# Stick-breaking values moved by one token: five transfers instead of two, and their differences ahead of the attention barrier

## The reference, cut to what matters

```python
log_keep = jnp.where(strict, jax.nn.log_sigmoid(-z), 0.0)
suffix = lax.cumsum(log_keep, axis=log_keep.ndim - 1, reverse=True) - log_keep
a = jnp.where(strict, jnp.exp(jax.nn.log_sigmoid(z) + suffix), 0.0)
return jnp.einsum('bhqs,bhsd->bhqd', a.astype(vh.dtype), vh)
```

## Time and profile before

| | us |
|---|---|
| median of 3 runs | 2915.65 |
| lowest and highest | 2914.1 and 2923.84 |
| profiled execution, its time | 2925.78 |
| profiled execution, its span | 2924.0 |
| PE busy in the span | 2787.3 (95%) |
| DVE busy | 1969.0 (67%) |
| ACT busy | 1158.3 (40%) |
| POOL busy | 99.9 (3%) |

### The profile page before, as it was taken

The page is one execution under the profiler, slowest core; times in us unless marked ns, Lnnn a source line. Parts: engine busy times, 40 slices in busy tenths (PEclk is TensorE's granted clock), DMA queues, the critical chain, the costliest instruction groups (busy, mean ns, idle before and its releaser), DMA issues.

```text
span 2924.0 us, 39546 instructions
## 1 busy us (share of the span) xinstructions
PE 2787.3 (95%) x15525; PEld 2269.3 (78%) x15525; DVE 1969.0 (67%) x3222; ACT 1158.3 (40%) x2049; POOL 99.9 (3%) x109
## 2 busy tenths in 40 slices
PE   6999988998999999999999999899979999999999
PEld 4878865677888776878888888778658788888887
DVE  6435215677446665487777787689975877777885
ACT  4334216633237785343333344411153433333443
POOL 1030001010320000000000000000000000000000
PEclk8999999998999998999999999899989999999999
DMA  7020210024100002222323563211002323325632
GB/s 282 17 85 22 65 38 15 10 93 128 43 12 2 2 1 94 93 96 106 116 102 107 206 223 101 65 51 44 17 30 99 105 101 108 115 101 206 223 94 101
DMA packets 187010, 257.31 MB, mean 88 GB/s; under 512 B 29736, under 2 KB 138700, under 8 KB 182220
## 3 DMA queue, kind: packets, MB, share of 16 engines
q1 hardware_dynamic: 182672, 232.45, 24.2%
q10 hardware_dynamic: 4155, 22.35, 1.9%
HBM read 186.62 MB, written 67.11 MB: 87 GB/s over the span
## 4 chain that ended last, share of the span: by engine, by line
PE 69%; DVE 7%; ACT 1%; issue 1%; DMA 0%; ACTq 0%; DVEq 0%
PE ps L1658 28%; PE ps L1666 14%; PE ps L1611 11%; PE ps L1434 4%; PE ps L1537 2%; PE ps L1488 2%; PE ps L1506 2%; PE ps L1722 2%; PE ps L1151 1%; PE ps L1773 1%; PE ps L1030 1%; PE ps L1759 0%; PE ps L1412 0%; DMA ring<-in_ffn_w_gate_dram 0%; DVE ht L2937 0%
## 5 line engine op out<-in xcount | busy, mean ns | idle before, releaser
L1658 PE MATMUL ps<-x_ops,w_ring 128*128 128x512 f32 x3696 | 841.9, 390 | 6.8 <-ACT even_rows L2287 5.3
L1658 PEld LDWEIGHTS ps<-x_ops,w_ring 128*128 128x128 f32 x3696 | 694.2, 188 | 152.6 <-issue 8.4
L1666 PE MATMUL ps<-a_ring,w_ring 128*128 128x512 f32 x1848 | 419.3, 389 | 0.0
L1666 PEld LDWEIGHTS ps<-a_ring,w_ring 128*128 128x128 f32 x1848 | 346.8, 188 | 72.2 <-DVE w_ring L3041 0.2
L1611 PE MATMUL ps<-h_high,ring_parts 128*128 128x512 f32 x1024 | 319.1, 393 | 19.0 <-DVE h_low L2509 9.8
L2229 ACT ACTIVATE w_ring<-ring 128x512 fp32r<-128x512 f32 x230 | 144.1, 628 | 302.7 <-PE ps L1658 284.8
L2472 DVE TENSOR_TENSOR ring_parts<-ring,ring_parts 128x1024 fp32r<-128x1024 f32 (+2 forms) x77 | 95.3, 1240 | 219.5 <-ACT ring_parts L1858 218.9
L1611 PEld LDWEIGHTS ps<-h_high,ring_parts 128*128 128x128 f32 x1024 | 192.6, 189 | 64.5 <-issue 12.9
L1611 PE MATMUL ps<-h_low,ring_parts 128*128 128x512 f32 x512 | 200.3, 391 | 0.0
L1858 ACT ACTIVATE ring_parts<-ring 128x1024 fp32r<-128x1024 f32 (+2 forms) x77 | 75.9, 989 | 277.2 <-PE ps L1611 177.2
L3041 DVE TENSOR_TENSOR w_ring<-ring,w_ring 128x512 fp32r<-128x512 f32 x230 | 158.0, 687 | 38.7 <-ACT w_ring L2229 38.7
(11 more groups left out here) (497 smaller groups left out, 4573.9 us busy)
## 6 DMA issues: line engine op xcount, KB each, us to landing
a_raw<-act_kept SPq DMA_DIRECT2D x70, 512.0 KB, 3.8
act_kept<-even_rows SPq DMA_DIRECT2D x12, 1536.0 KB, 5.1
act_kept<-odd_rows SPq DMA_DIRECT2D x10, 1536.0 KB, 5.1
ring<-in_ffn_w_gate_dram SPq DMA_DIRECT2D x12, 1024.0 KB, 5.8
ring<-in_ffn_w_up_dram SPq DMA_DIRECT2D x12, 1024.0 KB, 6.0
ring<-in_conv_w_pw_dram SPq DMA_DIRECT2D x24, 512.0 KB, 3.9
late<-in_ffn_w_gate_dram SPq DMA_DIRECT2D x10, 1024.0 KB, 5.8
late<-in_ffn_w_up_dram SPq DMA_DIRECT2D x10, 1024.0 KB, 6.1
```

What stands on the lines that cost most here:

```text
L1658: last = mm(o, w_ring[:, i % 4, wp_, P * k:P * k + P], x_ops[:, X_OP[p], rp_, k, :], start=p in "176" and k == 0 and p_ == 0, stop=k == 3 ...
L1666: last = mm(bank(OUT_BANK[DOWN_GROUP[p] + c_]), w_ring[:, (A_UNITS + b) % 4, wp_, P * c_:P * c_ + P], a_ring[:, b % 4, rp_, :], start=p in ...
```

## The change

The first of the two transfers moved 127 rows: partitions 0 to 126 to partitions 1 to 127. It becomes four, of 112, 8, 4 and 3 rows; the transfer that feeds partition 0 from partition 127 stays and now is the second of five. POOL's four operations on the moved values stand ahead of the barrier, and the mask `strict` behind it. The counts of `v_moved` follow: 80 for five transfers, 81 with POOL's mark.

```diff
-                    pe.wait_ge(s.v_moved, 33)
+                    pe.wait_ge(s.v_moved, 81)
...
-            load(v_step[1:P, :, :], sv[0:P - 1, :, :], s.v_moved)
+            load(v_step[16:P, :, :], sv[15:P - 1, :, :], s.v_moved)
             load(v_step[0:1, 1:TB, :], sv[P - 1:P, 0:TB - 1, :], s.v_moved)
+            load(v_step[8:16, :, :], sv[7:15, :, :], s.v_moved)
+            load(v_step[4:8, :, :], sv[3:7, :, :], s.v_moved)
+            load(v_step[1:4, :, :], sv[0:3, :, :], s.v_moved)
             high(T_AK + 2)
...
-            stage(g, "attention_in")
-            chain(g.memset(strict, 0.0))
-            select(strict[:, S - P:S], [[-1, P]], ALU.is_gt, 1.0, 0, 1).then_inc(s.const_ok, 1)
-            g.wait_ge(s.v_moved, 32)
+            g.wait_ge(s.v_moved, 80)
             chain(g.memset(v_step[0:1, 0, :], 0.0))
             chain(g.tensor_tensor(v_step, v_step, sv[:, :, :], ALU.subtract))
             chain(g.tensor_scalar(sv[:, :, :], sv[:, :, :], ident[:, P - 1:P], 1.0, ALU.mult, ALU.mult))
             g.tensor_tensor(sv[:, :, :], sv[:, :, :], v_step, ALU.add).then_inc(s.v_moved, 1)
+            stage(g, "attention_in")
+            chain(g.memset(strict, 0.0))
+            select(strict[:, S - P:S], [[-1, P]], ALU.is_gt, 1.0, 0, 1).then_inc(s.const_ok, 1)
```

## The result

| | before | changed |
|---|---|---|
| median of 5 runs, us | 2922.01 | 2898.93 |
| lowest and highest | 2914.1 to 2924.52 | 2896.63 to 2902.93 |
| profiled execution, time | 2925.78 | 2897.87 |
| profiled execution, span | 2924.0 | 2895.7 |

The ratio of the changed kernel to the one before is 0.9929, 95% interval 0.9913 to 0.9944: 0.71% faster, some 21 us, where 19.1 us (0.65%) were forecast. The median of before is 6.4 us above the 2915.65 from which the forecast was reckoned, now that two more runs are in it.

A forecast was written before the change was run, and what follows sets the result against it. PE, busy 95% of the span, was taken as the bound, so only its pauses and low clock could be won: 10.83 + 2.30 + 1.08 + 2.65 + 2.2 = 19.1 us off 2915.65 gives 2896.6 us, range 2890 to 2908.

The forecast's parts named there:

- The issue wait goes, 10.83 us, with 2.30 of clock and 1.08 ahead of SQ1: Ahead of the barrier, PE's pauses before SK1 and SQ1 and the half clock after the first go: 14.2 us earlier.
- The issues cost 2.8 us in all: On ACT, five transfer issues take 0.74 plus four times 0.52 us, freeing ACT at 384.7 instead of 401.03.
- no issue above 1 us: Sign to look for in the profile after: no single transfer issue on ACT takes over 1 us.
- The values land after 5 to 10 us: Moved values reach POOL at 387 to 392 us, where before it was about 424.
- POOL's chain has its place ahead of the barrier at no cost: POOL's 12.0 us of operations, ahead of the barrier, delay DVE but cost PE 0, with 2.4 us of slack.
- DVE is shut out for a whole chain: Rival, chance 0.10: ahead of the barrier, POOL's operations block DVE throughout, SQ0's low part is 4 us late; 2903 us.
- Behind the barrier 2.65 + 2.2 us: Behind the barrier, PE's 2.65 us pause before the first transpose goes, and 2.2 us from the clock staying full.
- The wait that I named as next late: Behind the barrier, PE's 0.70 us wait on the division for the third and fourth units, expected to stay.
- The gain is carried to the end: After the barrier everything follows PE, so the full 19.1 us gain reaches the kernel's end.
- The median of 2896.6 us: Whole kernel: the earlier median of 2915.65 less 19.1 us; the forecast case had chance 0.80.
- Not spread: Rival, chance 0.07: the 112-row transfer stays on one engine, ACT is free only at 396 to 401; 2911 us.
- Issues one by one: Rival, chance 0.03: each later transfer issue on ACT waits 18.42 us, PE stands 55 us longer; 2965 us, slower.

The follow-up runs named there:

- e1: Against the changed kernel: five transfers kept, POOL's four operations put back behind the barrier; ratio to the kernel before 0.9951.
- e3: Against the changed kernel: the 127 rows go as 113 and 14, three transfers in all; ratio to the kernel before 0.9987.
- e5: Against the changed kernel: the three small transfers become one of 15 rows, so three transfers of 112, 1 and 15; ratio to the kernel before 0.9940.
- e4: Against the kernel before: the high part of SK1 made ahead of the two transfer issues instead of behind them; ratio to the kernel before 0.9970.
- e2: Against the changed kernel: two transfers as before (127 rows and 1), POOL's four operations still ahead of the barrier; ratio to the kernel before 1.0005.
- e6: Against the changed kernel: ACT makes the high part of T_YM+1 behind the barrier instead of ahead of it; ratio to the kernel before 0.9925.
- e7: Against the changed kernel: the 127 rows go as 96 and 31, three transfers in all; ratio to the kernel before 0.9932.

## Why the prediction was right, by its own steps

- *The issue wait goes, 10.83 us, with 2.30 of clock and 1.08 ahead of SQ1.* 14.2 forecast, 14.51 measured. The 0.3 missing are two small losses. In an unbroken row a matmul starts 0.17 us before the end of the one ahead, and each of the two pauses lost that as well; I had counted it ahead of SQ1 alone. And SQ1, slow at its start, took 11.18 us from first to last matmul where SQ0 took 11.04. That the spreading carries this term is shown by e1, that it is the divisor by e3 against e5, and that the cost lies in ACT's order by e4.
- *The issues cost 2.8 us in all.* They cost 4.60. Each takes 0.6 to 0.7 us here, not 0.52, and the 8-row one took 1.88. My test "no issue above 1 us" was wrong. The slack of 5.6 us in the argument covered it: SK1's low part was ready at 381.67, and PE reached SK1 only at about 385.5.
- *The values land after 5 to 10 us.* 7.0 us. The transfers' time itself was mis-sized: ACT's DMA work took 3.1% of 16 engines over 120 us, 60 us of one engine, against 42 before. Spread, a row costs about 0.47 us of an engine and not 0.33. The 8 us more that the fixed cost of some 2 us per transfer would have added, one after the other, did not appear. The Trainium skill ("DMA: Bandwidth & Descriptors", "Anatomy of one DMA — SWDGE (gpsimd) path") gives that figure for transfers that GpSimd issues, and these are issued by ACT. They overlapped: in e5_112_15 all three landed 5.0 to 5.1 us after their issues, which are 0.6 us apart.
- *POOL's chain has its place ahead of the barrier at no cost.* Right, though it lasted 15.1 us with the collision, not 12.0. The low part of SQ0 was ready at 392.35 and wanted at about 396.4: 4.0 us of slack where I had worked out 2.4. Turns are taken, as e2 shows once more; that DVE is shut out for a whole chain is refuted in five profiles, those of the changed kernel, e2, e3, e5 and e6, where a DVE operation gets through inside POOL's chain. In e7 DVE met only the last operation of the chain, which tells nothing on this.
- *Behind the barrier 2.65 + 2.2 us.* 4.54 measured for 4.85. The pause and the half clock both went, as e2, e3, e5 and e7 repeat within 0.1 us. The two terms were off in opposite ways, and that the sum fits is in part luck. The wait that I named as next late stayed, and is two, 0.85 and 0.63 us against the 0.70 of before, so of the 2.65 only some 1.9 was won. The other 2.7 came from the clock, more than the 2.3 that I had as its upper bound.
- *The gain is carried to the end.* Yes: the timed difference is 20.7 us, with 16 to 25 as its interval, and the 19.05 lie inside. The 2.1 us behind "attended" are within the scatter of that stretch.
- *The median of 2896.6 us.* 2898.93 measured, but the closeness is in part luck. The base of 2915.65 was a median of three, low by 6.4 us against the 2922.01 of five; from that one the same sum gives 2902.9. And the lower end of the forecast's own range, 2892, does not follow from the terms that I gave for it: 0.7 and 1.6 below 2896.6 are 2894.3. What the runs bear out is the difference, not the absolute time.
- *The rivals.* "Not spread" is what e3 makes: it came out 3.8 us below before by its timing, where I had worked out 4.7 (2911 against 2915.65). "Issues one by one" is refuted by the changed kernel, where the four issues behind the first take 0.6 to 1.9 us, and by e3: its third issue, behind the same 113 rows on one engine, took 1.21 us at 395.9, some 26 us before the values were there.

## What to carry to other kernels

A wait of the busiest engine on a mostly idle one is worth following back queue by queue: here it went from PE over DVE and ACT to a DMA issue that stood behind a transfer on one engine. Look at the row count of a large transfer: here 127 and 113 rows went through one engine and 112 through sixteen, and the odd rest did no harm in a second transfer. Where an issue may have to wait, look at what stands behind it on its engine. Work that is moved out of a busy place is worth its move only if what it needs is there in time, so make the two edits together.

## What the runs showed of the hardware that I had not expected

- An issue behind a large one-engine transfer is let go long before that transfer is through: with 127 rows of 8 KB about 69 were left then, with 113 about 72 (an estimate, by 0.33 us a row from the first issue's start). That is not the whole of it. With 112 spread rows, 7 to an engine, the third issue still took 1.88 us in the changed kernel and 2.45 in e5, where the shortest took 0.6. Whether the limit is on one engine's queue or on all rows together no run tells.
- A pause can cost more than its length. The 2.65 us pause was followed by 7 us at half clock in the profile of before and by 10 in that of e1, and the 3.47 us pause of e4 by 7. In the other six profiles, where no pause ahead of the transposes is over 0.86 us, the clock is full. At the barrier it is less plain: 1.88 us of pause were followed by some 3 us at half clock in seven profiles and by none in that of e4, and 1.15 us by none in the one of e6.
- POOL's operation of 1.99 us takes 3.6 to 3.9 us when DVE's two-input operations stand against it, and DVE's operations of 1.2 us take up to 4.8: both lose, in turns.
- A transfer on one engine slows others that use this engine. The 512 KB raw tile of SQ1 took 22.8 us to land beside the 127 rows, 23.0 beside the 113, 11.4 beside the 31, and 3.8 in the changed kernel.
- 8 KB rows from SBUF to SBUF took 0.33 us each on one engine alone and about 0.47 us of an engine each when they were spread over up to sixteen (3.0 to 3.5% of 16 engines over the same 120 us in four profiles).
